# A weight stream in 1 MB pairs instead of 512 KB tiles, into the two halves of a four-slot ring

## What is computed (the reference)

```python
def reference(x, c, ctx, ..., c_2, ctx_2, ...):
    x = first_block(x, c, ctx, ...)      # modulate; p = h @ w_in; gated delta rule both ways over 8 heads
                                         # + chunked MLP mixer; (g_a*y_a + g_b*y_b) @ w_out; conv FFN 1024->2816->1024
    return second_block(x, c_2, ctx_2, ...)   # two layers: windowed + grouped attention, merge, w_out
```

## Time and profile before

| | |
|---|---|
| median of 3 runs | 2631.54 us (2630.66 to 2637.17) |
| the profiled execution | 2631.39 us |
| its span, first to last instruction | 2629.7 us |
| TensorE busy | 2578.9 us, 98% |
| the weight stream's queue (q1) | 153.11 MB, 17.1% of the DMA engines' time |
| issues of the stream | 288, 512 KB each, 3.8 us (median) to landing |

### The profile page before, as it was taken

How to read it: one execution, slowest core, us unless ns; L and a number is a source line. 1 busy time by engine, 2 the same in 40 slices (tenths; PEclk the granted TensorE clock), 3 DMA queues, 4 the chain that set the end, 5 groups by cost and what they waited for, 6 DMA issues and landing times.

```text
span 2629.7 us, 40325 instructions
## 1 busy us (share of the span) xinstructions
PE 2578.9 (98%) x15424; PEld 1910.9 (73%) x15424; DVE 1331.2 (51%) x2373; ACT 829.7 (32%) x1783; POOL 849.2 (32%) x716
## 2 busy tenths in 40 slices
PE   6899999999999999999999999999999999999999
PEld 2677777775788878888884567765555567778887
DVE  3455555553356568787842357533224513753324
ACT  3343444442312112222002347732111224663221
POOL 0222222220455535656543222012323034103444
PEclk8999999999999999999999999999999999999999
DMA  6211111113244434454322210001111122101222
GB/s 228 64 45 46 45 38 44 33 34 136 73 144 162 175 113 160 160 184 167 129 96 69 88 48 26 1 33 64 56 56 51 62 84 81 41 1 49 96 81 96
DMA packets 61410, 220.93 MB, mean 84 GB/s; under 512 B 6784, under 2 KB 8960, under 8 KB 60992
## 3 DMA queue, kind: packets, MB, share of 16 engines
q1 hardware_dynamic: 42576, 153.11, 17.1%
q0 software_dynamic: 14656, 56.89, 6.2%
q10 hardware_dynamic: 4016, 8.65, 0.9%
HBM read 214.90 MB, written 2.15 MB: 83 GB/s over the span
## 4 chain that ended last, share of the span: by engine, by line
PE 96%; DVE 2%; ACT 1%; DMA 1%; issue 1%; ACTq 0%; POOL 0%; DVEq 0%; SPq 0%
PE psum L456 92%; PE psum L960 3%; DMA arena<-in_stream 1%; PE psum L1018 0%; ACTq L1275 0%; PE psum L684 0%; ACT arena L1384 0%; PE psum L647 0%; POOL arena L2734 0%; DVE arena L2071 0%; DVE arena L2407 0%; DVE arena L2108 0%; ACT arena L1566 0%; DVE arena L2128 0%; ACT arena L1269 0%
## 5 line engine op out<-in xcount | busy, mean ns | idle before, releaser
L456 PE MATMUL psum<-arena 128*128 128x256 f32 (+10 forms) x14544 | 2476.4, 353 | 47.1 <-DVE arena L1756 12.3
L456 PEld LDWEIGHTS psum<-arena 128*128 128x128 f32 (+4 forms) x14544 | 1816.5, 170 | 689.1 <-issue 254.4
L2780 POOL TENSOR_TENSOR arena<-arena 128x512 f32<-128x512 f32 (+1 forms) x104 | 132.9, 1278 | 793.9 <-DMA arena<-in_stream 414.6
L2025 DVE TENSOR_TENSOR arena<-psum,arena 128x256 f32<-128x256 f32 (+1 forms) x103 | 47.3, 459 | 291.8 <-PE psum L456 283.6
L1996 DVE SCALAR_TENSOR_TENSOR arena<-arena 128x1024 f32<-128x1024 f32 x128 | 177.5, 1435 | 0.0
L2784 POOL TENSOR_TENSOR arena<-arena 128x512 f32<-128x512 f32 (+1 forms) x104 | 134.2, 1290 | 96.0 <-PE psum L456 90.2
L2031 DVE TENSOR_TENSOR arena<-psum,arena 128x256 f32<-128x256 f32 (+1 forms) x103 | 47.5, 461 | 227.2 <-PE psum L456 227.1
L2791 POOL TENSOR_TENSOR arena<-arena 128x512 f32<-128x512 f32 (+1 forms) x104 | 144.2, 1387 | 35.4 <-PE psum L456 35.1
L2788 POOL TENSOR_TENSOR arena<-arena 128x512 f32<-128x512 f32 (+1 forms) x104 | 135.2, 1300 | 44.1 <-PE psum L456 37.7
L1438 ACT ACTIVATE arena<-psum 128x256 f32<-128x256 f32 (+1 forms) x103 | 42.7, 415 | 305.0 <-PE psum L456 304.9
L2734 POOL TENSOR_TENSOR arena<-arena 128x512 f32<-128x512 f32 x16 | 22.1, 1401 | 315.1 <-ACT arena L1347 315.1
(11 more groups left out here) (281 smaller groups left out, 1823.0 us busy)
## 6 DMA issues: line engine op xcount, KB each, us to landing
arena<-in_stream SPq DMA_DIRECT2D x288, 512.0 KB, 3.8
arena<-in_mods POOLq DMA_DIRECT2D x80, 512.0 KB, 5.6
arena<-gc_rows POOLq DMA_DIRECT2D x16, 384.0 KB, 4.5
arena<-in_bias POOLq DMA_DIRECT2D x16, 384.0 KB, 3.8
arena<-in_xT ACTq DMA_DIRECT2D x2, 1024.0 KB, 13.8
arena<-in_conds ACTq DMA_DIRECT2D x1, 1536.0 KB
arena<-arena POOLq DMA_DIRECT2D x4, 384.0 KB, 4.3
out<-arena SPq DMA_DIRECT2D x3, 512.0 KB, 6.1
```

What stands on the lines that cost most here:

```text
L456: return pe.matmul(out, lhsT, rhs, start=start, stop=stop, skip_group_check=True)
L2780: add(sums[0], a21, a22, ALU.add).then_inc(s("wsum"), 1)
```

## The change

Each transfer now carries two neighbouring tiles, 1 MB, and fills one half of the ring: slots 0 and 1, or slots 2 and 3. In the source the two tiles lie 512 KB apart; the transfer's pattern keeps the 128 partitions as its first dimension, then the tile, then 1024 numbers. SyncE waits until both tiles of the half have been used. Readers of an odd tile wait for the semaphore of the even one; the numbers that they wait for stay the same.

```diff
-            for t in range(RING):
-                sp.dma_start(ring[:, t, :], a_stream[t]).then_inc(s(f"ring{t}"), 16)
+            for t in range(0, RING, 2):
+                sp.dma_start(ring[:, t:t + 2, :], a_stream[t:t + 2].rearrange("t p n -> p t n")).then_inc(s(f"ring{t}"), 16)
             with sp.Fori(1, T_ALL // RING) as i:
-                for t in range(RING):
-                    sp.wait_ge(s("used"), RING * i + t - (RING - 1))
-                    sp.dma_start(ring[:, t, :], a_stream[RING * i + t]).then_inc(s(f"ring{t}"), 16)
+                for t in range(0, RING, 2):
+                    sp.wait_ge(s("used"), RING * i + t - (RING - 2))
+                    sp.dma_start(ring[:, t:t + 2, :], a_stream[bass.ds(RING * i + t, 2)].rearrange("t p n -> p t n"))\
+                        .then_inc(s(f"ring{t}"), 16)
...
         def weights(pe, t, i=None, per=0):
 
             if i is None:
-                pe.wait_ge(s(f"ring{t % RING}"), 16 * (t // RING + 1))
+                pe.wait_ge(s(f"ring{t % RING // 2 * 2}"), 16 * (t // RING + 1))
             else:
-                pe.wait_ge(s(f"ring{t % RING}"), 16 * (t // RING + 1) + (16 * per // RING) * i)
+                pe.wait_ge(s(f"ring{t % RING // 2 * 2}"), 16 * (t // RING + 1) + (16 * per // RING) * i)
             return ring[:, t % RING, :]
```

## The result

The changed kernel is slower by little: 2636.85 us, the median of 19 runs (2634.23 to 2638.22), against 2632.17 us for 19 runs of the kernel before (2630.08 to 2637.17). The ratio is 1.0015, 95% interval 1.0009 to 1.0021: some 4 us (the medians stand 4.7 apart), within the 0.3% that was called "no change" ahead, yet clear of zero. The profiled execution took 2636.66 us, its span is 2635.0 us.

The account below looks back on a forecast made before the run. TensorE, busy for 2578.9 of 2629.7 us, was taken as the bound, except where it waits for the stream in the start. 2631.4 us (profiled execution) + 4.0 for the start = 2635.4, as median 2635.5; range 2631.4 to 2640.0.

Parts of the forecast that it names:

- Only the first 40 us can matter: Whole kernel: TensorE's 7.6 us of waits for the stream all lie before 39 us, in the first sixteen tiles.
- Landing of 1 MB: Any pair's transfer: lands in 4.9 us, wider bounds 4.2 to 6.0.
- The steps of the start: First sixteen tiles, pair by pair: the sixteenth starts at 42.7 us instead of 38.67, +4.0 us (+2.0 to +7.3).
- The cause as I gave it in a sentence: Start: one transfer in flight while TensorE works on the other half; first used slot empty until the second is used.
- It reaches the end whole: After tile 15: TensorE has nothing else to do, so the start's +4.0 us passes whole to the kernel's end.
- Value tiles: Tiles 52 and 53, issued at 632.1 us: pair lands at 641.9, 3 to 4 us of cover, costs nothing.
- Pairs and heads: Later stages: pairs need 4.9 us and are wanted after 8.6; heads have over 30 us of cover; both cost nothing.
- The rival of late pairs under contention: Steps with GpSimd's `in_mods` loads: pairs needing 9.0 us cost 0.4 in each of 35 steps, 14 us, total 2649; 8%.
- The bytes rival: Start: bound by bytes after all, so the whole loss is the first pair's 1.3 us, total 2632.7; 13%.
- Spreading: All pairs: two of 16 DMA engines carry each transfer, 22 us per 1 MB, over 1000 us in all; 1%.

Follow-up runs that it names:

- e1_single_start: Changed kernel with the first sixteen tiles one by one, all later ones in 1 MB pairs; 2631.26 us against 2632.92 for the kernel before.
- e2_pairs_start: Kernel before with the first sixteen tiles in 1 MB pairs, all later ones one by one; 2635.61 us against 2632.92.
- e5_delay: Kernel before plus three clears on VectorE in the lull after the sixteenth tile, no transfer changed; 2635.55 us against 2632.92.
- e7_half_release: Kernel before, but in the first sixteen tiles SyncE refills a half only when both tiles are used, by 512 KB transfers; 2633.36 us against 2633.40.
- e8_seen_together: Kernel before, but in the first sixteen tiles TensorE waits for both tiles of a pair before using the first; 2635.62 us against 2631.80.
- e9_both_halves: Kernel before with release and use by pairs in the first sixteen tiles, still two 512 KB transfers per pair; 2635.51 us against 2631.80.
- e3_deep_start: Changed kernel with tiles 0 to 9 sent to free room, so seven of eight first transfers need no wait; 2635.29 us against 2632.92 for the kernel before.

## Why the prediction was right, and where not

- *Only the first 40 us can matter.* Right, and shown: `e1_single_start` has no loss, and `e2_pairs_start` has it.
- *Landing of 1 MB: 4.9 us.* 5.0 (median of 44). The fit of the Trainium skill, "DMA: Bandwidth & Descriptors", section "Anatomy of one DMA — SWDGE (gpsimd) path", gave as an estimate 4.4; it is stated there for DMAs that GpSimd issues, and these are SyncE's. The measurement decides.
- *The steps of the start.* Forecast for tiles 4, 8, 12 and for the sixteenth: 22.0, 30.3, 38.1 and 42.7 us. Measured over the three profiles: 22.7 to 22.8, 29.9 to 30.0, 36.7 to 37.2, and 41.5 to 42.8. The forecast +4.0 met +3.7 at the mark and about 4 in the ratio. That it came so near is luck, since four steps were off, two each way. The first pair landed 7.5 us after its issue at 15.2, where 22.0 had supposed 6.8. From tile 4 to tile 8 it was 7.2 us instead of 8.3, and from 8 to 12 6.7 to 7.3 instead of 7.8: a pair is worked off in 2.0 us or less, and the next issue stands 1.8 to 2.2 us after its start, where I had reckoned 3.4 and 2.9 by taking one tile after the other. From tile 12 to tile 14 it was 4.4 to 4.7 us instead of 3.6: the norm sums ran at half the pace, which was nowhere in the sum. One reading was wrong, too: the 1.27 us from tile to tile, taken as the pace of products at the lower clock, is the pace of landings. Those rows say that TensorE waited for the stream before each, and in the second profile of before, at a granted clock of 1.00, the tiles that start at 28.80, 30.09 and 31.38 us stand 1.29 apart.
- *The cause as I gave it in a sentence* named a slot that stands empty until its neighbour is used. The sentence also has one transfer in flight while TensorE works on the other half; that is so, since of the issues at 24.9 and 27.4 us the first has landed at 29.95 and no third stands beside the second until 31.8. But the empty slot failed as a reason: alone it costs nothing that the runs can tell, 2633.36 us against 2633.40 (`e7_half_release`). The other part of my steps, that tile 4 waits for tile 5's landing and each landing counts 4.9 instead of 3.5, was in the sum but not in the sentence, and it brings the whole loss, 2635.62 us against 2631.80 (`e8_seen_together`). The sum took both, and the one brings the other with it. What the sum lacked is TensorE's slower pace.
- *It reaches the end whole.* Right as far as shown: `e5_delay` passes on 2.3 us as 2.6, with an interval of 0.3 to 5.0.
- *Value tiles.* The pair landed 9.8 us after its issue, as reckoned (641.9, plus the 4 us by which all had moved); cover left 4 us. *Pairs and heads:* no wait in the first profile, one of 0.4 and 0.6 us in the others, which kernels with single tiles have too. The rival of late pairs under contention: its largest landing is 7.5 us, where 8.6 would have been needed.
- *The bytes rival* is out: the share fell (0.73 against 0.87) and GB/s with it, 264 against 314. *Spreading* is out: landings of 5 us.

## What to carry to other kernels

A transfer that carries two tiles makes both wait for the later one, and where the reader catches up with the stream this coupling, not the rule for the refill and not the size, is the price: some 4 us over twelve tiles here. In the rows part of it is that the reader, which stands idle more, also runs at the lower pace for longer. Where the ring is ahead of its reader, the same halving of transfers is free, and gains nothing either. Before giving a starved start more room, look at what shares the DMA engines with it: weights asked for early pushed the inputs back by 12 us and took the gain away.

## What the runs showed of the hardware

- One transfer of 1 MB (two runs of 4 KB for each of 128 partitions, 512 KB apart in the source) lands in 5.0 us, two transfers of 512 KB issued 0.6 us apart in 5.1. SyncE's issue takes 372 ns for it, 333 before.
- Two profiles of one and the same kernel can differ by 3.2 us in span (2629.7 and 2632.9 for the kernel before) mostly by how long TensorE stays at 1.2 GHz after a lull (95 to 110 us: 0.92 or 0.72), and whether it falls there at all (925 to 940 us: 1.00 or 0.89). A difference of a few us between two single profiles has to be looked for there first.
- The granted clock of a stretch can read 1.00 while TensorE runs at half the pace: in `e8_seen_together` and `e9_both_halves` it is 1.00 from 36 to 42 us, and the weight loads of the norm sums stand 0.86 us apart, as in the changed kernel at 0.50, against 0.43 in the kernel before. The distance between like instructions is the surer sign.
- The size of one queue's transfers is felt in the issues of another: ScalarE's fourth early load takes 6.6 to 6.9 us to issue while SyncE's first transfers are of 512 KB (eight profiles) and 7.3 to 7.6 while they are of 1 MB (five), 9.2 with seven of 1 MB at once (`e3_deep_start`).
